# Masks on VectorE, and moved waits (gate tile, boundary, banded buffers, stick scores), in a two-layer hybrid decoder kernel

## The chip, the cores and the metric

The kernel runs on one core of a Trainium2 chip as one launch. The metric is the time of that launch on the device in microseconds (us). The core has TensorE (PE in the profile, its weight loads PEld), VectorE (DVE), ScalarE (ACT), GpSimd (POOL), and SyncE (SP), which here issues the loads of the weights. Each engine works through its own queue in order and waits at semaphores for the others.

## The reference

Two layers over 512 tokens of width 1024, float32. Each layer mixes tokens in three branches and then has an MLP:

```python
h = rms_norm(x, g_mix_pre);  proj = h @ w_in
o_a = mla_branch(...) @ w_o_mla            # 8 heads, causal: key <= query
o_b = swa_branch(...) @ w_o_swa            # 8 heads, window of 128 keys, one sink per head
o_c = stick_breaking_branch(...) @ w_o_sb  # 8 heads, key < query
mixed = gates[0] * o_a + gates[1] * o_b + gates[2] * o_c
x = x + rms_norm(mixed @ w_out, g_mix_post)
x = x + rms_norm(square(relu(rms_norm(x, g_mlp_pre) @ w_up)) @ w_down, g_mlp_post)
```

In the causal branch `s = where(key <= query, s, -inf)` and a softmax over the keys. In the banded branch a query sees the keys of its own block of 128 up to itself, and of the block before it those less than 128 away; the softmax has the exponential of the sink in its denominator. The masks of these two branches are what the change moves.

## The kernel before, in words

**Layout and precision.** Activations lie transposed, channels on the 128 partitions and the 512 tokens along the row. Each float32 matrix product is made of three passes over rounded operands (`three`): high with high, low with high, high with low. The high half of an operand is a copy in the rounded type (`..._hi`, ScalarE), the low half is what the copy lost, a subtraction on VectorE (`..._lo`). Weights come in chunks of 128 x 1024: a load, then `split` on ScalarE (L1053) and on VectorE (L1600). One output tile of 128 x 512 is 24 matmuls of 512 columns (`tile`, 8 steps over k of three passes each).

**What sets the order.** Nothing is planned at run time: the function `order()` at the head of the file lists the tiles in TensorE's order, which gives each tile its PSUM bank by turns (a few banks rotate) and each weight chunk its place in the ring. A tile waits for the release of the bank by the tile that had it before (`take_bank`, `free_of`). Apart from that list each engine's program is written out by hand; the change edits these by hand too.

**Causal heads.** For each head h: TensorE makes the scores, keys on the partitions and queries along the row, in the causal shape only (1280 columns in three banks: 512, 512 and 256), and adds the mask at the end of each bank by a matmul of the identity with a constant (`causal_mask`, L604; the mask is -BIG above the diagonal). VectorE takes the maximum over the key blocks (`biggest`, L1711 and L1713), GpSimd reduces it over the partitions, TensorE subtracts it from the scores (`mla_shift`), ScalarE takes the exponentials (`soft_exp`, L1137) and copies the high half (`soft_hi`, L1144), VectorE makes the low half (`probs_lo`, L1690), and TensorE multiplies with the values (`values`, which wait for the low half). The denominator comes out of the same matmul as further rows of the bank `pv_bank`; ScalarE takes ln and exp of it (L1108, L1110), VectorE multiplies (`soft_out`, L1722, writes `of` and gives the bank free). TensorE's order in round h is: scores of h+1, query projection of h+2, values of h, then a tile of 24 matmuls (a gate tile in most rounds) in whose middle the maximum of h+1 is subtracted. VectorE's order in round h is: maximum h+1, query of h+2, `soft_out` h, a weight split, in layer 0 a part of the angles of the rotary table (`angle_turns`, `angle_less`, `angle`, `angle_ahead`, after heads 0 to 3), low half h+1, scaling of a gate tile. After head 4, in layer 0, ScalarE makes the sines of that table (`table_sin`, with two table loads).

**Banded heads.** The eight heads run in four pairs (t = 0 to 3), with TensorE's scores of a whole pair made together (`band_scores`): two banks a head, 512 and 384 columns, masks of 512 columns for the first and of 256 and 128 for the second, for each head of the pair. Two buffers hold the exponentials (`bs_f`), one each the high and the low half (`bp_hi`, `bp_lo`). The denominator is the sum with the sink on VectorE (`band_den`, L1803), then as above. Beside it run output tiles (`o`), the rotation of the next queries (`rope_in`, `rope_turn`: L1776, L1781, L1788, L1791, L1793) and the scaling of the stick-breaking inputs (`stick_scaled`). The values of a head wait for the bank `pv_bank`, which the head before gives free with its `of`.

**Stick-breaking heads** follow. Their first step is `stick_scores(0)` on TensorE, then the clamp on VectorE (`stick_min`, L1840), and exponentials, logarithms and sums on the way to `stick_tail`.

**Boundary.** At the end of layer 0 the last down tiles are made in halves of 256 tokens. `down_part` adds a tile to `y` (L1964) and squares it for the norm (`gather`, L1616, with a square of ScalarE, L1070), while the first tiles of layer 1 start as soon as banks and inputs are free.

## Time and profile before

| | |
|---|---|
| three runs | 1720.91 us median, 1720.56 to 1721.05 |
| profiled execution, its own time | 1720.57 us |
| its span | 1718.8 us |
| TensorE busy | 1693.2 us, 99% |
| VectorE busy | 1117.5 us, 65% |
| ScalarE busy | 852.8 us, 50% |
| GpSimd busy | 150.8 us, 9% |
| granted TensorE clock, mean | 0.998 |

The span is the profiled execution from its first to its last instruction; its own time is a little more. Busy times count the instructions that do work; matmuls are pipelined, so that two starts of 512 columns lie 0.23 us apart although one takes 0.39 from start to end. L12 is line 12 of the kernel. In a timeline a row may stand for several instructions of a line (x2), and the bracket tells how long the engine was idle before it and what ended that.

### The profile page before, as it was taken

To read this page: it belongs to the slowest core of one execution; us is meant where nothing else is said; L and a number is where in the kernel's file an instruction comes from. 1 tells how busy PE (TensorE), PEld (TensorE's weight loads), DVE (VectorE), ACT (ScalarE), POOL (GpSimd) and SP (SyncE) were. 2 spreads that over 40 slices of the span, in tenths; PEclk is the share of its full clock that TensorE was granted. 3 is DMA by queue.
4 is the path that set the end of the run, shared out by engine and by line. 5 is a ranking of instruction groups with operands and counts; after the bars stand their busy time and mean duration, and the time that the engine had idled before them with its cause. 6 is when DMAs were issued, how large, how long until landed. Compare 5 with 4: busy or idle time off the path is not lost.

```text
span 1718.8 us, 21730 instructions
## 1 busy us (share of the span) xinstructions
PE 1693.2 (99%) x8533; PEld 1429.0 (83%) x8533; DVE 1117.5 (65%) x1530; ACT 852.8 (50%) x1204; POOL 150.8 (9%) x142
## 2 busy tenths in 40 slices
PE   8999999999999999999999999999999999999997
PEld 6888888888898888888888888888888988888886
DVE  8887888886566534364597777888754765344545
ACT  7576566665455424131466755666644553231223
POOL 0111211111100000000001111111111000000000
PEclk9999999999999999999999999999999999999999
DMA  4121122222332222222321211122224222222222
GB/s 151 66 71 60 62 69 75 78 74 86 135 111 85 93 94 97 99 98 98 120 83 65 77 62 62 62 74 74 74 92 161 78 90 96 98 98 98 98 98 74
DMA packets 47495, 152.02 MB, mean 88 GB/s; under 512 B 5153, under 2 KB 9633, under 8 KB 47394
## 3 DMA queue, kind: packets, MB, share of 16 engines
q1 hardware_dynamic: 45664, 147.36, 24.7%
q10 hardware_dynamic: 1730, 3.28, 0.5%
q8 instruction: 68, 1.11, 0.3%
q14 instruction: 33, 0.27, 0.0%
HBM read 146.42 MB, written 4.19 MB: 88 GB/s over the span
## 4 chain that ended last, share of the span: by engine, by line
PE 83%; issue 6%; DVE 5%; ACT 3%; POOL 1%; DMA 1%; SPq 0%; DVEq 0%; POOLq 0%; ACTq 0%
PE bank L599 78%; PE bank L604 2%; PE bank L856 1%; PE bank L901 1%; POOL mix L2342 1%; ACT w_hi L1053 1%; DVE w_lo L1600 1%; POOL fb L2372 1%; PE bank L703 0%; DMA x<-in_x 0%; DVE hf L1647 0%; ACT dn L1110 0%; ACT dn L1108 0%; DVE h_lo L1635 0%; DVE of L1722 0%
## 5 line engine op out<-in xcount | busy, mean ns | idle before, releaser
L599 PE MATMUL bank<-h_hi,w_hi 128*128 128x512 f32 (+1 forms) x1224 | 477.3, 390 | 6.4 <-DVEq L1739 2.8
L599 PE MATMUL bank<-h_hi,w_lo 128*128 128x512 f32 (+1 forms) x1224 | 471.9, 386 | 0.0
L599 PE MATMUL bank<-h_lo,w_hi 128*128 128x512 f32 (+1 forms) x1224 | 471.6, 385 | 0.0
L1053 ACT ACTIVATE w_hi<-raw 128x1024 fp32r<-128x1024 f32 (+2 forms) x269 | 270.5, 1013 | 206.4 <-DMA raw<-in_w 205.9
L1600 DVE TENSOR_TENSOR w_lo<-raw,w_hi 128x1024 fp32r<-128x1024 f32 (+2 forms) x269 | 316.3, 1179 | 59.5 <-ACT w_hi L1053 52.7
L599 PEld LDWEIGHTS bank<-h_hi,w_hi 128*128 128x128 f32 x1224 | 230.1, 188 | 55.5 <-issue 6.2
L599 PEld LDWEIGHTS bank<-h_hi,w_lo 128*128 128x128 f32 x1224 | 229.9, 188 | 47.1
L599 PEld LDWEIGHTS bank<-h_lo,w_hi 128*128 128x128 f32 x1224 | 230.2, 188 | 44.8 <-issue 1.2
L599 PE MATMUL bank<-u_hi,w_hi 128*128 128x512 f32 (+1 forms) x560 | 208.0, 371 | 0.0
L599 PE MATMUL bank<-u_hi,w_lo 128*128 128x512 f32 (+1 forms) x560 | 207.7, 371 | 0.0
L599 PE MATMUL bank<-u_lo,w_hi 128*128 128x512 f32 (+1 forms) x560 | 207.7, 371 | 0.0
L599 PEld LDWEIGHTS bank<-u_hi,w_hi 128*128 128x128 f32 x560 | 105.5, 188 | 18.3
L599 PEld LDWEIGHTS bank<-u_lo,w_hi 128*128 128x128 f32 x560 | 105.5, 188 | 18.2
L599 PEld LDWEIGHTS bank<-u_hi,w_lo 128*128 128x128 f32 x560 | 105.5, 188 | 18.0
L1934 DVE TENSOR_TENSOR usq<-relu 128x512 f32<-128x512 f32 x64 | 44.2, 691 | 101.7 <-ACT relu L1258 101.2
L1258 ACT ACTIVATE relu<-bank 128x512 f32<-128x512 f32 x48 | 28.6, 595 | 136.5 <-PE bank L599 136.5
L1952 DVE TENSOR_TENSOR y<-bank,y 128x512 f32<-128x512 f32 x32 | 22.1, 691 | 98.7 <-PE bank L599 98.7
L599 PE MATMUL bank<-o_hi,w_hi 128*128 128x512 f32 x192 | 76.6, 399 | 0.0
L1260 ACT ACTIVATE u_hi<-relu 128x512 fp32r<-128x512 f32 x64 | 40.5, 633 | 70.1 <-DVE relu L1929 68.6
L599 PE MATMUL bank<-o_hi,w_lo 128*128 128x512 f32 x192 | 75.0, 390 | 0.0
L2342 POOL TENSOR_TENSOR mix<-mix,gate 128x512 f32<-128x512 f32 x32 | 44.4, 1390 | 346.5 <-DVE gate L1909 346.5
L599 PE MATMUL bank<-o_lo,w_hi 128*128 128x512 f32 x192 | 74.8, 390 | 0.0
(267 smaller groups left out, 2738.7 us busy)
## 6 DMA issues: line engine op xcount, KB each, us to landing
raw<-in_w SPq DMA_DIRECT2D x251, 512.0 KB, 3.2
x<-in_x SPq DMA_DIRECT2D x16, 256.0 KB, 3.5
side_raw<-in_w SPq DMA_DIRECT2D x6, 512.0 KB, 4.9
x_spill<-x ACTq DMA_DIRECT2D x8, 256.0 KB, 2.2
x<-x_spill SPq DMA_DIRECT2D x8, 256.0 KB, 3.0
out_y<-x SPq DMA_DIRECT2D x8, 256.0 KB, 2.1
raw<-in_w SPq DMA_DIRECT2D x8, 192.0 KB, 2.4
raw<-in_w SPq DMA_DIRECT2D x8, 128.0 KB, 2.3
```

Source lines behind the costliest of these rows:

```text
L599: mm = pe.matmul(o, s, m, start=start and i == 0 and j == 0, stop=last and i == n - 1 and j == 2, skip_group_check=True)
L604: return pe.matmul(o, stationary, moving, start=False, stop=True, skip_group_check=True)
L856: return pe.matmul(to[:, off + col:off + col + w], a, m, start=(r, n, i) in STICK_STARTS, stop=i == 2, skip_group_check=True)
L901: mm = pe.matmul(pv_bank[:, q0:q0 + w], v[:, j, h % 2, :], part[:, s], start=i == 0 and part is p_hi, stop=part is p_lo, skip_group_check= ...
L1053: act.activation(chunk_in(gc, w_hi, side_hi)[:, 0:w], chunk_in(gc, raw, side_raw)[:, 0:w], ACT.Copy)\
L1258: act.activation(relu[:, n % 2, :], tile_bank(name)[:, :], ACT.Relu).then_inc(free_of(name), 1)
L1260: act.activation(u_hi[g % 2][:, t, :], relu[:, n % 2, :], ACT.Square).then_inc(u_h.sem, 1)
L1600: dve.tensor_tensor(chunk_in(gc, w_lo, side_lo)[:, 0:w], chunk_in(gc, raw, side_raw)[:, 0:w], chunk_in(gc, w_hi, side_hi)[:, 0:w].bitcast( ...
L1934: dve.tensor_tensor(usq[:, n % 2, :], relu[:, n % 2, :], relu[:, n % 2, :], ALU.mult)\
L1952: ins = dve.tensor_tensor(y[:, t, :], tile_bank(name)[:, :], y[:, t, :], ALU.add)
L2342: pool.tensor_tensor(mix[:, t, :], mix[:, t, :], gated_at(b, t), ALU.add).then_inc(mix_add.sem, 1)
L2372: pool.tensor_tensor(to, to, tri01[:, :], ALU.mult).then_inc(z_mask.sem, 1)
```

## The change

- **Masks.** In causal heads the mask matmul of the first bank goes. The first maximum is taken in two steps, 128 columns with the mask added and a copy of 384. After the exponentials VectorE takes the minimum of the first 128 columns with a constant `bound`, which is 0 where a key is later than the query and large elsewhere (`causal_masked`), and ScalarE's high half waits for it (`p_mask`). In banded heads half of the mask columns go (512 to 256 in the first bank; the 256-column masks in the second), the first two maxima add the mask, and `band_masked` takes the minimum over two stretches of 256 columns.
- **Gate tile.** The tile ("gate", 0, 2) is taken before the last of four value tiles; `mla_shift(0)` stands before its k-tile 6 in place of 4. The queues of ScalarE and VectorE follow: `split` of the next gate chunk after head 0's halves, scaling of the gate tile before them.
- **Banded buffers.** `bp_hi` and `bp_lo` become two each, the low half written over the exponentials. ScalarE's high half of the odd head moves ahead of the rotation and the stick inputs. VectorE's minimum and low half of the odd head move into `rope_turn`, ahead of its last subtraction, and with that ahead of the stick scaling and of the denominator of the even head.
- **Stick scores.** `stick_scores(0)` is issued inside the tile ("stick_vt", 0), after its first k-tile, and no longer before it.
- **Boundary.** At the end of layer 0 the sum of tile (5, half 1) stays in its place on VectorE, its `gather` moves behind `layer_lo(0, 0)`, and ScalarE's part of it behind the second `next_in`.

```diff
 order():                                       # TensorE's tiles
-        elif h == 1:
-            seq += values[-1:]
         if 0 < h < HEADS - 1:
             seq += own("gate", 0, h + 1)
+        if h == 1:
+            seq += values[-1:]
...
+        bound = place("bound", [P, 2 * P], F32)
-        bp_hi = place("bp_hi", [P, BANDED_COLS], F32R, r3 + 5632)
-        bp_lo = place("bp_lo", [P, BANDED_COLS], F32R, r3 + 9216)
+        bp_hi = [place(f"bp_hi{s}", [P, BANDED_COLS], F32R, r3 + 5632 + 3584 * s) for s in range(2)]
+        bp_lo = [place(f"bp_lo{s}", [P, BANDED_COLS], F32R, r3 + 16896 * s) for s in range(2)]
+        bp_lo_last = place("bp_lo_last", [P, BANDED_COLS], F32R, r1 + 16384 + 10240)
...
 PE, scores():
-                            causal_mask(to, off, b, MASK_CAUSAL).then_inc(score_full.sem, 1)
+                            if b:
+                                mm = causal_mask(to, off, b, MASK_CAUSAL)
+                            mm.then_inc(score_full.sem, 1)
 PE, band_scores():
-                                    mm = add(band[r][0][:, :].rearrange("p (a c) -> p a c", a=2), cst[:, IDENT, :],
-                                             both.unsqueeze(1).broadcast_to([P, 2, 2 * P]))
+                                    mm = add(band[r][0][:, 2 * P:4 * P], cst[:, IDENT, :], both)
                                 else:
-                                    add(band[r][1][:, 0:2 * P], cst[:, IDENT, :], both)
                                     mm = add(band[r][1][:, 2 * P:3 * P], cst[:, IDENT, :], cst[:, MASK_CAUSAL, :])
 PE, order of the work:
+                    tile(("gate", 0, 2), h_hi, h_lo, None, lambda: mla_shift(0), half=KT - 2)
                     mla_v(NB - 1)
-                    tile(("gate", 0, 2), h_hi, h_lo, None, lambda: mla_shift(0))
...
-                    stick_scores(0)
-                    tile(("stick_vt", 0), h_hi, h_lo)
+                    tile(("stick_vt", 0), h_hi, h_lo, None, lambda: stick_scores(0), half=1)
 ACT, soft_exp() and soft_hi():
-                        act.wait_ge(*p_l(n if n <= HEADS else n - 1))
+                        act.wait_ge(*(pv_full(n - 1) if n > HEADS + 1 else p_l(min(n, HEADS))))
...
+                    act.wait_ge(*p_mask(n + 1))
+                    read = n - 1 if n > HEADS else n
+                    if read > 0:
+                        act.wait_ge(*pv_full(read))
 ACT, start of the heads:
-                    mla_q(1)
-                    mla_v(NB - 1)
                     for j in range(NB - 1):
                         mla_v(j)
+                    mla_q(1)
                     soft_exp(0)
+                    mla_v(NB - 1)
+                    soft_hi(0, s_f[:, :], p_hi[:, :])
                     split(C["gate", 0, 2] + 2)
-                    soft_hi(0, s_f[:, :], p_hi[:, :])
 ACT, banded pairs:
                         sink_exp(n)
+                        band_hi(n + 1)
                         if t < 2:
                             rope_out(t + 3, wq_hi[:, t + 2, :])
...
-                        band_hi(n + 1)
 DVE, biggest():
-                            ins = dve.tensor_scalar(to[:, q0:q0 + w], src, floor, None, ALU.max)
+                            ins = dve.scalar_tensor_tensor(out=to[:, q0:q0 + w], in0=src, scalar=floor, in1=both,
+                                                           op0=ALU.max, op1=ALU.add)
                         elif i == 0:
-                            ins = dve.tensor_copy(to[:, q0:q0 + w], src)
+                            dve.tensor_tensor(to[:, 0:P], src[:, 0:P], cst[:, MASK_CAUSAL, :].bitcast(F32), ALU.add)
+                            ins = dve.tensor_copy(to[:, P:SEQ], src[:, P:SEQ])
+                def causal_masked(h):
+                    dve.wait_ge(*p_exp(banks_of(h) + 1))
+                    dve.tensor_tensor(s_f[:, 0:P], s_f[:, 0:P], bound[:, 0:P], ALU.min).then_inc(p_mask.sem, 1)
+                def band_masked(n):
+                    dve.wait_ge(*p_exp(banks_of(HEADS + n + 1)))
+                    halves = bs_f[n % 2][:, 0:6 * P].rearrange("p (a c) -> p a c", a=3)[:, 0:3:2, :]
+                    dve.tensor_tensor(halves, halves, bound[:, :].unsqueeze(1).broadcast_to([P, 2, 2 * P]), ALU.min)
+                       .then_inc(p_mask.sem, 1)
 DVE, start of the heads:
                     mla_q(1)
+                    mla_v(0)
+                    mla_qk(1)
+                    for j in range(1, NB - 1):
+                        mla_v(j)
+                    causal_masked(0)
+                    scaled(("gate", 0, 2), mix[:, 2, :])
                     mla_v(NB - 1)
-                    mla_qk(1)
-                    for j in range(NB - 1):
-                        mla_v(j)
+                    probs_lo(0, s_f[:, :], p_hi[:, :], p_lo[:, :])
                     split(C["gate", 0, 2] + 2)
-                    probs_lo(0, s_f[:, :], p_hi[:, :], p_lo[:, :])
-                    scaled(("gate", 0, 2), mix[:, 2, :])
 DVE, round h, after the angle operations:
                         if h + 1 < HEADS:
+                            causal_masked(h + 1)
                             probs_lo(h + 1, s_f[:, :], p_hi[:, :], p_lo[:, :])
 DVE, banded pairs:
+                        band_masked(n)
                         band_lo(n)
...
-                            rope_turn(t + 3, ("swa_q", t + 2), wq_lo[:, t + 2, :], wq_hi[:, t + 2, :])
+                            rope_turn(t + 3, ("swa_q", t + 2), wq_lo[:, t + 2, :], wq_hi[:, t + 2, :],
+                                      lambda: second_low(n + 1))      # band_masked, band_lo
+                        else:
+                            second_low(n + 1)
                         if t == 0:
-                            rope_in(4, ("swa_q", 3), 0.125)
-                        elif t < 3:
-                            stick_scaled(0, t - 1)
-                        band_den(n)
-                        band_lo(n + 1)
+                            rope_in(4, ("swa_q", 3), 0.125, lambda: band_den(n))
+                        else:
+                            if t < 3:
+                                stick_scaled(0, t - 1)
+                            band_den(n)
 DVE, end of layer 0:
-                            down_part(HALF, 1)
+                            down_sum(HALF, 1)                          # its gather after layer_lo(0, 0)
```

## Rows read from the trace of the kernel before

**Rows 1.** The page's busy times: us, share of the span, instructions.
```profile
PE 1693.2 (99%) x8533; PEld 1429.0 (83%) x8533; DVE 1117.5 (65%) x1530; ACT 852.8 (50%) x1204; POOL 150.8 (9%) x142
```

**Rows 2.** TensorE's waits: us in total, times, longest us.
```profile
PE bank L599 <- DVE h_lo L1635: 4.0, 4, 1.4
PE bank L599 <- DVEq L1739: 2.8, 2, 1.4
PE bank L599 <- DVE of L1722: 1.9, 6, 0.5
```

**Rows 3.** Timeline of TensorE, gate tile: start us, us, [idle before <-releaser].
```profile
55.19 0.39 PE L599 MATMUL bank<-w_lo,ckn_hi 128*128 128x512 f32 x1
55.42 0.40 PE L599 MATMUL bank<-w_hi,ckn_lo 128*128 128x512 f32 x1
57.22 0.47 PE L599 MATMUL bank<-h_hi,w_hi 128*128 128x512 f32 x1 [1.40 <-DVEq L1739]
```

**Rows 4.** The same timeline, scores of head 2 with the mask.
```profile
88.06 0.22 PE L604 MATMUL bank<-cst 128*128 128x128 f32 x1
88.12 0.39 PE L599 MATMUL bank<-mq_hi,mk_hi 128*128 128x384 f32 x1
88.35 0.34 PE L599 MATMUL bank<-mq_lo,mk_hi 128*128 128x384 f32 x1
```

**Rows 5.** The same, masks of a band pair and the values behind.
```profile
185.74 0.73 PE L604 MATMUL bank<-cst 128*128 128x512 f32 x2
...
187.24 0.68 PE L604 MATMUL bank<-cst 128*128 128x256 f32 x4
188.43 0.36 PE L599 MATMUL bank<-bp_hi,wv_hi 128*128 128x256 f32 x1 [0.51 <-DVE of L1722]
```

**Rows 6.** VectorE's groups by form: busy us, mean ns, idle before us.
```profile
L1934 DVE TENSOR_TENSOR usq<-relu 128x512 f32<-128x512 f32 x64 | 44.2, 691 | 101.7 <-ACT relu L1258 101.2
...
L1690 DVE TENSOR_TENSOR p_lo<-s_f,p_hi 128x1280 fp32r<-128x1280 f32 x16 | 23.9, 1492 | 17.1 <-ACT p_hi L1144 16.8
...
L1690 DVE TENSOR_TENSOR bp_lo<-bs_f,bp_hi 128x896 fp32r<-128x896 f32 x16 | 17.5, 1092 | 6.2 <-ACT bp_hi L1144 6.1
...
L1861 DVE TENSOR_TENSOR later_f<-later_f 64x128 f32<-64x128 f32 x16 | 4.5, 284 | 0.6
```

**Rows 7.** Timeline of VectorE, low halves of heads 1 and 2.
```profile
75.85 1.49 DVE L1690 TENSOR_TENSOR p_lo<-s_f,p_hi 128x1280 fp32r<-128x1280 f32 x1 [0.21 <-ACT p_hi L1144]
...
87.29 1.49 DVE L1690 TENSOR_TENSOR p_lo<-s_f,p_hi 128x1280 fp32r<-128x1280 f32 x1 [0.54 <-ACT p_hi L1144]
```

**Rows 8.** Timeline of ScalarE, high half of head 1.
```profile
74.47 1.27 ACT L1144 ACTIVATE p_hi<-s_f 128x1280 fp32r<-128x1280 f32 x1
```

**Rows 9.** Timeline of TensorE, values of head 1.
```profile
79.36 0.40 PE L599 MATMUL bank<-p_hi,mv_hi 128*128 128x512 f32 x1
```

**Rows 10.** Timeline of ScalarE, behind the gate of head 4.
```profile
125.51 1.28 ACT L1058 ACT_TABLE_LOAD   x1
```

**Rows 11.** Timeline of VectorE, banded stage and the first stick clamp.
```profile
176.14 1.09 DVE L1690 TENSOR_TENSOR bp_lo<-bs_f,bp_hi 128x896 fp32r<-128x896 f32 x1 [0.57 <-ACT bp_hi L1144]
...
182.12 0.69 DVE L1793 TENSOR_TENSOR wq_lo<-ra,wq_hi 128x512 fp32r<-128x512 f32 x1 [0.70 <-ACT wq_hi L1170]
184.22 0.69 DVE L1776 SCALAR_TENSOR_TENSOR rp_lo<-bank,rp_hi 128x512 fp32r<-128x512 f32 x1 [1.41 <-ACT rp_hi L1166]
...
203.89 0.69 DVE L1803 TENSOR_TENSOR dn<-bank,dn 64x512 f32<-64x512 f32 x1 [0.67 <-PE bank L599]
...
220.97 0.69 DVE L1682 TENSOR_TENSOR tmp<-bank,rstd_x 128x512 f32<-128x512 f32 x1 [2.43 <-PE bank L599]
...
239.60 0.67 DVE L1840 TENSOR_SCALAR fb<-bank 128x512 f32<-128x512 f32 x1
```

**Rows 12.** Timelines of VectorE and GpSimd, an add beside a reduction.
```profile
167.94 1.05 DVE L1791 TENSOR_TENSOR ra<-ra,rb 128x512 f32<-128x512 f32 x1
...
167.40 1.78 POOL L2331 PARTITION_ALL_REDUCE bmxr<-bmx  x1 [22.53 <-DVE bmx L1713]
```

More of the change, by code:

```diff
@@ L124 @@
 VECS = V_SINK + HEADS
-IDENT, SWAP, NEG_TRI, NEG_ONE, ONE, MASK_CAUSAL, MASK_PREV, NEG_PART, TRI_MOST = range(9)
-N_CONST = 9 * P
+IDENT, SWAP, NEG_TRI, NEG_ONE, ONE, MASK_CAUSAL, MASK_PREV, NEG_PART, TRI_MOST, BOUND = range(10)
+N_CONST = 11 * P
 TRIG = 4 * 4
@@ L453, in banks_of, with band_low @@
             return 3 * n if n < HEADS else 2 * n + HEADS
+        def band_low(n):
+            return bp_lo_last if n == HEADS - 1 else bp_lo[n % 2]
         def chunk_of(name):
@@ L638, in weight, with tile @@
                     return (chunk_in(gc, w_hi, side_hi)[:, rows], chunk_in(gc, w_lo, side_lo)[:, rows])
-                def tile(name, hi, lo, ready=None, halfway=None, cols=ALL):
+                def tile(name, hi, lo, ready=None, halfway=None, cols=ALL, half=KT // 2):
                     c = chunk_of(name)
@@ L647, in tile @@
                             pe.wait_ge(*ready[0](ready[1] + t + 1))
-                        if halfway and t == KT // 2:
+                        if halfway and t == half:
                             halfway()
@@ L727, in scores @@
                         to, off = banks[b]
-                        three(to[:, off + col:off + col + w], [(keys(j), queries(q0, w))], start=off + col == 0)
+                        mm = three(to[:, off + col:off + col + w], [(keys(j), queries(q0, w))], start=off + col == 0)
                         if n + 1 == len(pieces) or pieces[n + 1][3] != b:
-                            causal_mask(to, off, b, MASK_CAUSAL).then_inc(score_full.sem, 1)
+                            if b:
+                                mm = causal_mask(to, off, b, MASK_CAUSAL)
+                            mm.then_inc(score_full.sem, 1)
                 def less_biggest(n, pieces, banks, biggest_):
@@ L1315, in _ @@
                     .then_inc(const_set, 1)
+                act.activation(bound[:, :], cst_f[:, BOUND * P:(BOUND + 2) * P], ACT.Copy).then_inc(const_set, 1)
                 table_sin(2, QPE, 2, slice(HEAD, P))
@@ L1714, in biggest @@
                         ins.then_inc(mx_step.sem, 1)
+                def causal_masked(h):
+                    dve.wait_ge(const_set, 4)
+                    dve.wait_ge(*p_exp(banks_of(h) + 1))
[3 more added lines that the diff above has]
+                    halves = bs_f[n % 2][:, 0:6 * P].rearrange("p (a c) -> p a c", a=3)[:, 0:3:2, :]
+                    dve.tensor_tensor(halves, halves, bound[:, :].unsqueeze(1).broadcast_to([P, 2, 2 * P]), ALU.min)\
+                       .then_inc(p_mask.sem, 1)
                 def soft_out(n):
@@ L1766, in mla_biggest, with rope_in @@
                     biggest(h, CAUSAL, score, mx)
-                def rope_in(n, name, scale):
+                def rope_in(n, name, scale, between=None):
                     dve.wait_ge(*rp_h(n + 1))
@@ L1778, in rope_in @@
                            .then_inc(rp_l.sem, 1)
+                    if between:
+                        between()
                     if n:
@@ L1782, in rope_in, with rope_turn @@
                                              op0=ALU.mult, op1=ALU.mult).then_inc(free_of(name), 1)
-                def rope_turn(n, name, dst, hi):
+                def rope_turn(n, name, dst, hi, between=None):
                     dve.wait_ge(*rot(n + 1))
@@ L1791, in rope_turn @@
                     dve.tensor_tensor(ra[:, :], ra[:, :], rb[:, :], ALU.add).then_inc(rp_sum.sem, 1)
+                    if between:
+                        between()
                     dve.wait_ge(*rpo_h(n + 1))
@@ L1836, in stick_min @@
                             dve.wait_ge(*p_l(2 * HEADS + max(h - 1, 0)))
+                            if h == 0:
+                                dve.wait_ge(*pv_full(2 * HEADS - 1))
                             if h < 2:
@@ L1965, in down_part @@
                        .then_inc(free_of(name), 1)
+                def down_part(t, h):
+                    down_sum(t, h)
                     gather(MPOST, t, h)
@@ L2306, in layer_lo, with first_lo_gather @@
                         next_lo(t, (4 + h) * KT + t + 1, vec(V_PRE + t, layer=now[0] + 1), HALVES[h])
+                    def first_lo_gather(t, h):
+                        layer_lo(t, h)
+                        if t == 0:
+                            gather(MPOST, HALF, 1)
                     for p in range(KT // 2 + 1):
-                        residual(p, 0, KT, layer_lo if more else None)
+                        residual(p, 0, KT, (first_lo_gather if p == 1 else layer_lo) if more else None)
                         if p == 0:
-                            down_part(HALF, 1)
+                            down_sum(HALF, 1)
+                            if not more:
+                                gather(MPOST, HALF, 1)
                         elif p == 1:
```

27 lines of the change are left out of this document (18 added, 9 removed).

## The prediction, made before the changed kernel was seen

> **What bounds the kernel now.** I read four views in this order. First the busy times of the page: TensorE is at work for 1693.2 of 1718.8 us [rows 1], so it is the bound almost everywhere, and an edit gains only by taking columns off TensorE or by ending one of its waits. Then the waits of TensorE by releaser [rows 2]: the reader is to see that they are few and short: 2.8 us in two waits behind VectorE's L1739 (the gate tile, one a layer), 1.9 us in six behind the head output of L1722 (banded stage), 4.0 us in four behind L1635, the longest of 1.4 us at the boundary between layers. All that this change aims at is in those rows and in the mask matmuls. Third the timeline of TensorE at these places [rows 3 to 5]. Last, VectorE's and ScalarE's queues around a head [rows 6 to 11], because the change moves work onto VectorE and makes ScalarE wait for it; there it must be seen how much idle time VectorE has before the operation that TensorE waits for.
>
> The sum is made against the profiled execution: 1720.57 us, span 1718.8 and 1.8 around it. The median of the runs shown is 1720.91, 0.3 more, which I leave out.
>
> **The gate tile.** In both layers TensorE starts the last value matmul at 55.42 and the gate tile at 57.22: 1.80 where 0.23 is the pace (55.19 to 55.42) [rows 3], so 1.57 lost, and some 0.07 of restart. With the order swapped the tile takes the bank that is free and the value matmul the one freed late, by then long free. Gain 1.64 a layer at that point. What hides the moved work: `shift(0)` moves from before k-tile 4 to before k-tile 6, where its maximum is ready. The price is in VectorE's queue: the scaling of the gate now stands before the low half of the probabilities of head 0, and a weight split of 1.2 us behind it, so head 1's work on VectorE starts some 0.3 to 0.6 later than before, while TensorE comes 1.64 earlier.
>
> **Causal masks, TensorE's side.** The mask of bank 0 starts at 88.06 and the next matmul at 88.12, 0.06; the 384-column matmul behind it takes 0.23 to the next [rows 4], where three quarters of the 0.23 of 512 columns are 0.17: some 0.05 for the switch. 0.11 a head, 0.88 a layer, 1.76 for 16.
>
> **Causal masks, the other side.** The first maximum becomes a masked add of 128 columns and a copy of 384, about 0.2 more on VectorE. The new minimum on 128 columns costs 0.29 (L1861) [rows 6]. What counts is its place: ScalarE's high half now waits for it, and it stands in VectorE's queue behind the weight split and, in layer 0, behind the angle operations of heads 1 to 4. In the trace of before those ran beside ScalarE's high half: for head 1 it ran from 74.47 to 75.74 [rows 8], VectorE's last angle operation ended at 75.64, and the low half started at 75.85 after 0.21 idle [rows 7]. After: angle operation to 75.64, minimum to 75.93, high half 1.27, low half at about 77.3, so 1.45 later, and 0.3 more from the queue of the gate tile: 1.75. Low half to 79.1; TensorE wants it at 79.36 less 1.97 of lead (1.64, and three masks) = 77.4 [rows 9]. The lead is gone at head 1, stall 1.7.
>
> Heads 2, 3 and 4 repeat it, since VectorE goes from head to head almost without idle time: each adds the high half and the minimum less the idle time VectorE had before the low half (0.54 at head 2 [rows 7]; heads 3 and 4 repeat the pattern of head 1 with as little), so 1.1, 1.5 and 1.5. VectorE is 1.75 + 4.1 = 5.9 late at head 4. TensorE had 2.0 of slack there (low half of head 1 ended at 77.34, wanted at 79.36 [rows 7, 9]), but in the next round ScalarE stands with two table loads and the sines from 125.51 on [rows 10] behind the gate, right before the exponentials of head 6, and that stretch had no slack: the lateness passes whole. Term for layer 0's causal stage, gate gain and mask cuts in it: bounds +3.8 (the slack holds) and +6.3, and below nothing if the lead survives (−2.5, a rival below). I take +6.0.
>
> In layer 1 there are no angle operations. The minimum costs 0.3 beside the exponentials, the gate queue's 0.4 stays. TensorE stalls some 0.4 once and then keeps the rest: −1.64 − 0.88 + 0.4 = −2.15; bounds −2.5 and 0.
>
> **Banded stage.** TensorE loses masks: of two 512-column and four 256/128-column ones (0.73 and 0.68 [rows 5]) some 0.5 a pair, 4 us in all by name. But each pair's next matmul waits for `of` anyway (0.51 at 188.43 [rows 5]), a chain over the denominator on VectorE, so I credit none of it by itself. On that chain stand, new: the minimum of 512 elements, 0.61 from start to start (0.69 alone, L1934 [rows 6]), twice a pair, ScalarE's high half of 0.95 behind each, and the low half of 1.09 [rows 6], which now stands *before* the denominator and not after it. The idle time in VectorE's queue pays a part.
> - Pair 0: the low half of band head 0 started at 176.14 [rows 11]; now the minimum ends at 176.1, high half to 177.1, low half 1.05 later. Then, before the low half of the rotated query, 0.70 of idle time at 182.12 goes and 0.61 + 1.0 + 1.02 come: 3.0 later in all. The idle 1.41 before 184.22 [rows 11] pays half, and one operation of 0.6 to 0.7 moves behind the denominator. Denominator at 186.3 for 185.54: +0.76 at the head's `of`, on which TensorE stands.
> - Pair 1: +1.5 at the even low half and the same 1.9 behind it, paid by the idle 0.67 before 203.89 [rows 11], and by the odd high half that no longer delays the denominator's exponential on ScalarE: +1.4.
> - Pair 2: the same, but VectorE had 2.43 idle at 220.97 [rows 11]: +0.36.
> - Pair 3: both low halves stand before the denominator and `of`, behind which stick-breaking's first clamp starts: 239.60 [rows 11] becomes 243.3. The stick chain behind it has waits of its own, and I let it pay a little over half, as in pair 0: +1.70, bounds 0 and +3.7.
>
> The moved stick scores (inside the tile, after its first k-tile) take a 0.6 wait of TensorE away before that last step, so it only changes where the same lateness is felt: zero; bounds −0.6 and 0. Double buffers let the exponentials and the high half start earlier, but the low half still waits for the minimum, which waits its turn: zero by itself. Sum of the stage: +4.2 a layer, 8.5 for both. Bounds: −1.5 a layer (VectorE hides all, the 1.9 of `of` waits [rows 2] go) and +5.5.
>
> **Boundary.** The wait at L1635 of 1.4 us [rows 2] ends when a down tile's sum is done; the change moves one gather, whose square comes from ScalarE, out from ahead of it. Bounds 0 and −1.4; I take −0.6, once.
>
> **Start-up.** One more copy of 256 columns on ScalarE and 128 KB more of constants, before the first matmul needs either: 0, bounds 0 and +0.3.
>
> **Sum.** 6.0 − 2.15 + 8.5 − 0.6 = +11.8: 1720.57 + 11.8 = 1732.4 us.
>
> **One rule against it.** The row: an add of two SBUF inputs (L1791) that started at 167.94, 0.54 after GpSimd's reduction of 167.40, took 1.05 where its kind takes 0.69 [rows 12, 6]; so it was slowed by 0.36, yet ended inside the reduction's 1.78. Both inputs of the banded minimum are in SBUF, and for even heads it would start 0.4 to 1.2 us into such a reduction. As a mechanism of this kernel: 4 such minima a layer, each 0.36 to 1.2 later, on the denominator's chain, 8 × 0.36 = 2.9 to 8 × 1.2 = 9.6, of which part stays in slack: 1735 to 1741 us.
> The Trainium skill, page "SBUF — State Buffer", section "SBUF: two separate sides", says that VectorE and GpSimd share a pair of ports under an exclusive lock, and that a VectorE operation with two SBUF inputs is fully blocked while a GpSimd operation that reads SBUF holds it. By that rule the add of 167.94 would have ended no earlier than 169.2 + 0.7; the trace has 168.99, so it agrees in direction and not in size.
>
> **Rivals.**
> - *VectorE hides the masks* (faster). If the low halves stay inside the 2.0 us of slack at head 1 and in the banded stage's idle times, TensorE keeps everything: −3.3 gate, −1.8 causal masks, −4 band masks and `of` waits at most, −0.6: 1711 to 1713 us. For it: VectorE is busy 65% on average. Against it: at heads 1 and 2 of layer 0 it was idle for 0.21 and 0.54 before the low half [rows 7], less than one high half. It decides at the low half of head 1: if that starts before 76 us, this one holds.
> - *The band stage is neutral* (slower, less). The low half before the denominator costs nothing because double buffers pull the exponentials ahead; then 6.0 − 2.15 − 0.6 = +3.3, 1723.8. For it: pair 2's idle of 2.43. Against: the minimum waits for its turn in VectorE's queue.
> - *Layer 0 keeps the slack*: 3.8 for 6.0, 1730: inside the forecast's own range.
> - *The ports*, above: 1735 to 1741.
> - *The change doesn't do what it says*: the waits move and the masks' cost equals their gain, 1720 to 1721.5.
>
> **Chances.** Forecast with its own range of 1726 to 1737: 0.62. Neutral band stage 0.14. Ports 0.11. VectorE hides it 0.09. No change 0.04. The range takes in the forecast, most of the neutral band stage and the lower part of the ports: 1723 to 1738. Faster by over 0.2% (3.4 us, about what can be told from no change): 0.09; within it: 0.07 (0.04, and 0.03 from the low end of the neutral band stage); slower: 0.84.
>
> **What would show it.** Right: the low half of head 1 starts at 77 or later, and TensorE's waits have new rows behind `p_lo` L1690 in layer 0 alone, some 8 us in all; no wait behind L1739; waits behind `of` grow from 0.5 to over 1 us; the first clamp is 3 to 4 us late against the values of band head 6. Wrong: `p_lo` waits absent or the denominators at their old distance from the band scores. If the causal stage of layer 0 is no longer than before, the queue of angle operations was misjudged; if the clamp is not late, the banded chain was.

## The result and the profile after

The changed kernel takes 1749.47 us (median of 4 runs, 1748.81 to 1750.73) against 1720.98 for the kernel before on the same chip (4 runs, 1720.56 to 1721.65): ratio 1.0167, 95% interval 1.0155 to 1.0179, or 28.5 us slower. Forecast were 11.8 us. The profiled execution is the one of 1750.73 us, span 1748.9; the one of before had 1718.8. So the two traces lie 30.1 us apart, and the sums below are made between them.

The page's busy times and TensorE's waits after (us in total, times, longest), which answer to [rows 1] and [rows 2]:

```profile
PE 1701.2 (97%) x8501; PEld 1434.5 (82%) x8501; DVE 1133.1 (65%) x1578; ACT 853.9 (49%) x1205; POOL 151.0 (9%) x142
...
PE bank L605 <- DVE of L1746: 12.1, 6, 2.8
PE bank L605 <- DVEq L1763: 5.6, 2, 3.0
PE bank L605 <- DVE h_lo L1644: 2.8, 3, 1.8
PE bank L605 <- DVE bp_lo L1699: 2.6, 2, 1.4
PE bank L610 <- DVE sp_lo L1903: 2.5, 2, 1.2
PE bank L605 <- DVE mix L1691: 2.4, 1, 2.4
```

The waits for the head output went from 1.9 to 12.1 us, those behind the query's release from 2.8 to 5.6, and three groups are new. TensorE's busy time has also grown, by 8.0 us, with 32 matmuls less. The granted clock tells why. The next fence is TensorE's timeline at the tile gate(0, 3) of layer 0, and then a table by stretches (us; busy time and count of PE, PEld, DVE, ACT, POOL; granted clock; DMA share; GB/s):

```profile
70.51 0.77 PE L605 MATMUL bank<-h_hi,w_hi 128*128 128x512 f32 x1 [2.59 <-DVEq L1763]
...
71.00:76.00 5.00, 5.00 (x13) 3.87 (x12) 4.42 (x7) 3.48 (x7) 0.59 (x1) 0.50 0.00 0
78.00:80.00 2.00, 2.00 (x11) 1.65 (x10) 0.80 (x1) 1.97 (x3) 0.00 (x0) 1.00 0.00 0
200.00:202.00 2.00, 2.00 (x9) 1.81 (x8) 1.33 (x4) 0.19 (x1) 1.36 (x1) 0.50 0.00 0
```

After a wait of 2.59 us the granted clock is 0.50 for 5 us, that is 1.2 GHz and not 2.4, and then 1.00 again. That is so too behind the wait of 2.43 us for the head output at 198.77.

**Where the 30.1 us went.** I matched the same matmuls in both traces and took how much later each starts. The column on half clock is what the lateness grew by from the first to the last matmul of each stretch at half pace (0.43 us from start to start for 512 columns and 0.21 for 256, where 0.23 and 0.12 are the pace). The first matmul behind a wait is in it, so some tenths of it are restart and not clock.

| stage | later at its end | gained in it | of that half clock | the rest | forecast |
|---|---|---|---|---|---|
| layer 0, causal heads (to 164.9 of before) | 8.9 | 8.9 | 2.9 | 6.0 | 6.0 |
| layer 0, banded and stick (to 258.3) | 19.8 | 10.9 | 4.3 | 6.6 | 4.2 |
| to the heads of layer 1 (902.3) | 19.2 | -0.6 | 0 | -0.6 | -0.6 |
| layer 1, causal heads (1014.1) | 21.9 | 2.8 | 1.6 | 1.2 | -2.15 |
| layer 1, banded and stick (1107.5) | 30.2 | 8.3 | 1.6 | 6.7 | 4.2 |

Of the 16.7 us between the forecast and the measured loss the two banded stages are the greater part: 19.2 us were lost there where 8.5 were forecast.

### The profile page after: what moved, and what is told of

Same layout as the page of the kernel before. It is cut to its first block, busy times and chain, and to the rows that moved or that the text cites. A ratio compares the mean times of both kernels' runs of the same rounds, so it can differ in the third digit from the quotient of the medians.

```text
span 1748.9 us, 21737 instructions
## 1 busy us (share of the span) xinstructions
PE 1701.2 (97%) x8501; PEld 1434.5 (82%) x8501; DVE 1133.1 (65%) x1578; ACT 853.9 (49%) x1205; POOL 151.0 (9%) x142
## 3 DMA queue, kind: packets, MB, share of 16 engines
q8 instruction: 68, 1.11, 0.3%
## 4 chain that ended last, share of the span: by engine, by line
PE 66%; issue 9%; DVE 9%; ACT 6%; POOL 1%; DMA 0%; DVEq 0%; POOLq 0%; ACTq 0%
PE bank L605 63%; ACT w_hi L1058 1%; PE bank L610 1%; ACT bp_hi L1151 1%; DVE w_lo L1609 1%; PE bank L862 1%; PE bank L907 1%; POOL mix L2395 1%; DVE bp_lo L1699 1%; DVE bmx L1719 1%; DVE dn L1831 1%; ACT p_hi L1151 1%; POOL fb L2425 0%; ACT dn L1115 0%; DVE mx L1726 0%
```

## The experiments

Each run has its own runs of the kernel before on the same chip (medians 1720.4 to 1720.9). The ratio is given with its 95% interval.

| run | what it is | median us | ratio |
|---|---|---|---|
| e1 | changed, gate tile part undone | 1747.67 | 1.0153 [1.0138, 1.0168] |
| e2 | changed, masks on TensorE | 1722.30 | 1.0010 [1.0000, 1.0019] |
| e3 | changed, old banded order | 1757.12 | 1.0209 [1.0193, 1.0224] |
| e4 | changed, TensorE kept busy in the banded waits | 1745.46 | 1.0143 [1.0128, 1.0158] |
| e5 | changed, masks on TensorE and gate part undone | 1718.47 | 0.9987 [0.9978, 0.9996] |
| e6 | before with the gate part alone | 1725.92 | 1.0031 [1.0019, 1.0042] |
| e7 | before with one load later | 1724.64 | 1.0023 [1.0014, 1.0032] |
| e8 | e5 with causal masks on VectorE | 1726.22 | 1.0034 [1.0022, 1.0046] |
| e9 | e5 with banded masks on VectorE | 1739.71 | 1.0108 [1.0095, 1.0122] |
| e10 | e8, minimum ahead of the angles | 1720.22 | 0.9997 [0.9988, 1.0006] |
| e11 | e9, odd minimum earlier | 1729.94 | 1.0051 [1.0038, 1.0065] |
| e12 | e5, query of head 1 between the maxima | 1717.03 | 0.9977 [0.9968, 0.9986] |
| e13 | e9, TensorE kept busy | 1734.28 | 1.0079 [1.0064, 1.0094] |
| e14 | e11, denominator before the odd low half | 1722.98 | 1.0018 [1.0008, 1.0027] |

The parts put together: e5 is -2.3 us against its runs of before, causal masks (e8 less e5) +7.75, banded masks (e9 less e5) +21.2, gate tile in their company (changed less e1) +1.8. The sum is 28.5, the measured loss 28.5. That they agree to the tenth is chance: e1's four runs lie between 1743.95 and 1749.44, and the intervals of e1 and of the changed kernel overlap. What is tested by it is that causal and banded masks add up: e5 and both costs give 1747.5, and e1, which has both, took 1747.67. The gate part does not add up. It costs 1.8 us beside both masks (e1), 3.8 without them (e2 less e5) and 5.2 alone in the kernel before (e6).

### The gate tile: e1, e6, e7

e1 takes the part out of the changed kernel, e6 puts it alone into the kernel before; the diff is that of the part shown above, undone or done.

> The changed kernel with its gate tile part undone (order of the tiles, place of the maximum, queues of ScalarE and VectorE at the start of the heads); all other parts stay. Theory: the swap keeps the value chunk of the weights in use until after the gate tile, the next chunk's load starts 6 us later, and through VectorE's queue the tile gate(0,3) of each layer waits 2.6 to 3.0 us for its bank, after which TensorE ran at half clock for 5 to 6 us. Undoing it takes away about +3.2 of lag at that place in layer 0 and +2.9 in layer 1: 1743 to 1744 us. Rival: the gate swap gains its 1.6 a layer as I forecast and the lateness comes from the masks in VectorE's queue: then undoing it costs, 1751 to 1753 us.

> The kernel before with the gate tile part alone (tile order, place of the maximum, the queues at the start of the heads). Theory: the 1.57 us wait goes and a longer one comes at gate(0,3), with half clock behind it in some executions: +2.5 and +1.3 us, 1723.5 to 1726 us. Rival (my forecast): -1.6 a layer, 1717.7 us.

e7 is the kernel before with one wait on SyncE:

```diff
                         sp.wait_ge(*full(LAST[gone % CHUNKS] + 1))
+                        if gone % CHUNKS == C["mla_v",]:
+                            sp.wait_ge(*shift(1))
```

> The kernel before with one wait more on SyncE: the load that takes the place of the value chunk of the weights waits until head 0's maximum is subtracted (about 5 us later than before, where the changed kernel starts it). Nothing else is moved. Theory: the late load alone makes VectorE's split late, with it the maxima of head 1 and the query of head 2, whose bank gate(0,3) waits for: a wait of 1.5 to 3 us appears behind the query's release (L1739) at 69.6 and at its place in layer 1: 1724 to 1729 us. Rival: it is the changed order of VectorE's queue and not the load: 1720.5 to 1722 us.

Alone the part costs 5.2 us (e6), where the forecast had a gain of 3.3. Why stands in the trace of the changed kernel; first the loads of weights with their first and last start between 50 and 70 us, before and after, then ScalarE's and VectorE's timelines after:

```profile
L582 SPq DMA_DIRECT2D raw<-in_w x4: 327/328/432, 55.8 to 67.9; - x4
```

```profile
L588 SPq DMA_DIRECT2D raw<-in_w x4: 328/379/431, 61.8 to 66.1; - x4
...
65.14 1.06 ACT L1058 ACTIVATE w_hi<-raw 128x1024 fp32r<-128x1024 f32 x1 [1.54 <-DMA raw<-in_w]
...
66.23 1.23 DVE L1609 TENSOR_TENSOR w_lo<-raw,w_hi 128x1024 fp32r<-128x1024 f32 x1 [1.11 <-ACT w_hi L1058]
...
69.63 0.68 DVE L1761 TENSOR_TENSOR mqf<-bank,tab 128x512 f32<-128x512 f32 x1
```

The load of the next weight chunk started at 55.8 and now at 61.8. It goes into the place in the ring that the value chunk leaves, and SyncE waits for the last tile that reads it. That is the last value tile, which the swap puts behind the gate tile's 24 matmuls. ScalarE then stands 1.54 us for the load and VectorE 1.11 for ScalarE, the maxima of head 1 and the query of head 2 come 1.4 us later, and gate(0, 3) uses the bank of that query (two banks rotate): TensorE, 1.6 ahead, waits 2.59 where it waited for nothing. e7, which only starts that load later, costs 3.9 us without any other edit, as the theory had it in size. It missed the place: the wait of 1.53 us stands at the key matmul of head 2, behind the gate tile's scaling (`mix`), which in e7 still stands at its old place in VectorE's queue. So the late load by itself is shown to cost most of what e6 costs. That in the changed kernel it works through the bank of head 2's query is read from the trace above; no run has the new queue without the late load. The half clock is on top: e6's trace has it behind both of its long waits, e7's behind none.

In the changed kernel the part costs only 1.8 (e1), less than the expected 5.5 to 6.5, and its rival, that undoing the part costs, fell too. In layer 0 the later waits of the masks, which are for the same engine, take the lateness in: the changed kernel's trace is 3.3 us behind e1's at 80 us and 1.0 behind at 105. In layer 1 it is 4.1 behind at the end of the causal heads and 1.3 at the end of the banded stage, where e1 had two stretches of half clock (1.6 and 2.9 us) and the changed kernel one (1.6). So a part of the small 1.8 is chance of the clock.

### The masks: e2, e5, e8, e9

e2 puts all masks back on TensorE in the changed kernel; e5 undoes the gate part too; e8 and e9 are e5 with one kind of mask on VectorE.

> The changed kernel with all masks on TensorE again (causal and banded), no minimum on VectorE and no wait of ScalarE for it; gate swap, banded buffers and order, stick scores and boundary stay. Theory: masks on VectorE cost about 8 us in layer 0's causal heads and some 4 us in the banded stages; the rest is the gate tile and the banded order: 1735 to 1739 us. Rival: the masks are the whole loss: 1718 to 1722 us. Second rival: they cost nothing, 1748 to 1754 us.

> The changed kernel with the masks back on TensorE and the gate tile part undone; what is left of the change is banded buffers and order, stick scores and boundary. Theory: masks on TensorE brought 1722.3, and the gate tile there still cost 2.5 us in layer 0 and 1.3 in layer 1 at the first head after it, so without it 1718 to 1719 us: a version under the kernel before. Rival: the gate tile's lateness is made up later in any case: 1720.5 to 1722.5 us.

> As the one with neither masks on VectorE nor gate tile part, but with the causal masks of bank 0 on VectorE. Theory: layer 0's angle operations with the minimum behind them cost 6 to 8 us there, layer 1 costs 0 to -1: 1724 to 1727 us. Rival: the lateness is the maxima's (two steps for one) and comes in both layers alike: 1720 to 1722 us in all, or the same in both layers.

> As the version with neither masks on VectorE nor gate tile part (1718.5), but with the banded masks on VectorE. Both masks together on it gave 1747.7 and the causal ones 1726.2. Theory: the parts add up, so the banded masks alone cost some 21 us, about 10.7 a layer, of which 3 to 4 a layer are half clock behind the long waits for the head output: 1738 to 1741 us. Rival: the two only cost that much together, because the causal masks make the banded stage start late: under 1733 us.

My expectation for e2 fell and its rival stood: the masks are the whole loss. What is left of the change without them and without the gate part is a gain of 2.3 us (e5). The causal masks cost 7.75 us (e8), all in layer 0. At the end of its causal heads e8's trace is 7.9 us behind that of the kernel before, 1.6 of them a stretch of half clock at 121.7, and over the causal heads of layer 1 the lag is 6.7 at the start and at the end. The low halves tell why. In layer 1 of the kernel before VectorE was idle for 1.5 to 2.1 us ahead of those of heads 1 to 7, more than the 1.39 it is idle in e8, so the round trip to ScalarE fits in. At heads 1 to 4 of layer 0 it had 0.15 to 0.54. The banded masks cost 21.2 (e9), and by themselves: beside the causal ones they cost the same (e1 less e8, 21.45).

### Where the causal minimum stands: e10

```diff
                             split(C["swa_q", 0] + 2)
+                        if h + 1 < HEADS:
+                            causal_masked(h + 1)
                         if now[0] == 0:
                             if h == 0:
                                 angle_turns(1)
...
                         if h + 1 < HEADS:
-                            causal_masked(h + 1)
                             probs_lo(h + 1, s_f[:, :], p_hi[:, :], p_lo[:, :])
```

> The version with the causal masks alone on VectorE (1726.2), with the minimum moved ahead of the angle operations of layer 0 in VectorE's queue, behind the weight split. Theory: the 7.9 us of layer 0 come from the high half that waits behind the angles; with the minimum ahead it starts 0.3 after the exponentials and runs beside the angles again: 1717.5 to 1719 us. Rival: the minimum and the longer maxima are what VectorE's queue can't hold in layer 0, wherever they stand: 1722 us or more.

6.0 of the 7.75 us go with the place of one operation of 0.29 us, the half clock behind the wait of 2.37 us among them. VectorE's timeline at head 1, e8 and then e10, which answers to [rows 7]:

```profile
75.98 0.43 DVE L1586 TENSOR_SCALAR tt<-tt 128x512 f32<-128x512 f32 x1
76.44 0.29 DVE L1733 TENSOR_TENSOR s_f<-s_f,bound 128x128 f32<-128x128 f32 x1
78.12 1.49 DVE L1702 TENSOR_TENSOR p_lo<-s_f,p_hi 128x1280 fp32r<-128x1280 f32 x1 [1.39 <-ACT p_hi L1154]
```

```profile
75.07 0.28 DVE L1733 TENSOR_TENSOR s_f<-s_f,bound 128x128 f32<-128x128 f32 x1
...
76.82 1.49 DVE L1702 TENSOR_TENSOR p_lo<-s_f,p_hi 128x1280 fp32r<-128x1280 f32 x1
```

In e8 the low half starts 1.39 us after VectorE is free, behind ScalarE's high half; in e10 the high half ran beside the angles and the low half waits for nothing. 1.75 us stay, and the expected 0 did not come: half a microsecond in head 4's round and 1.2 at the values of head 6 of layer 0. What makes these is open; the longer maxima (0.28 + 0.55 for 0.68) are my guess.

### Where the banded minimum and low half stand: e3, e11, e14

e3 is the changed kernel with the old order on VectorE and ScalarE (the odd head's minimum and low half after `band_den`, its high half after the rotation); e11 is e9 with the odd minimum ahead of `mixed`; e14 is e11 with the denominator first:

```diff
 e11
+                        band_masked(n + 1)
                         mixed(n + 1)
...
                 def second_low(n):
-                    band_masked(n)
                     band_lo(n)
 e14, besides
-                            rope_turn(t + 3, ("swa_q", t + 2), wq_lo[:, t + 2, :], wq_hi[:, t + 2, :],
-                                      lambda: second_low(n + 1))
-                        else:
-                            second_low(n + 1)
+                            rope_turn(t + 3, ("swa_q", t + 2), wq_lo[:, t + 2, :], wq_hi[:, t + 2, :])
...
                             band_den(n)
+                        band_lo(n + 1)
```

> The changed kernel with the old order of the banded pairs: VectorE takes the odd head's minimum and low half after the rotation, the stick scaling and the even head's denominator, ScalarE the odd high half after rotation and stick inputs; masks stay on VectorE, buffers stay double. Theory: the waits of TensorE behind the head output (2.4 to 2.8 us, two a layer) come from the denominator standing behind the odd low half; undone, they fall under 1 us and the half clock behind them goes: 10 to 14 us less, 1736 to 1740 us. Rival: the minimum itself makes the lateness, wherever it stands: 1746 us or more.

> The version with the banded masks alone on VectorE, with the odd head's minimum moved ahead of the mixing of the output tile, so that ScalarE's high half is done when VectorE comes to the low half. Theory: the round trip (1.07 us idle before each low half) at the odd heads goes, four a layer, and the waits for the head output become shorter by 1 us each: 5 to 9 us under the banded masks alone, clock included. Rival: the even heads' round trip and the work itself make the lateness: 0 to 3 us less.

> The version with the banded masks on VectorE and the odd head's minimum early (1729.9), with the even head's denominator taken before the odd head's low half. Theory: since the high half is ready early, the low half no longer idles VectorE, and the 1.0 us of it ahead of the denominator is what is left of the waits for the head output: 3 to 6 us less, 1724 to 1727 us. Rival: as with the late minimum (where the old order cost 7.6 more), the low half after the denominator makes the next head late: 1730 to 1735 us.

VectorE's timeline in the first pair of the changed kernel, to be held against [rows 11]:

```profile
184.37 1.16 DVE L1737 TENSOR_TENSOR bs_f<-bs_f,bound 128x512 f32<-128x512 f32 x1
186.61 1.09 DVE L1699 TENSOR_TENSOR bp_lo<-bs_f,bp_hi 128x896 fp32r<-128x896 f32 x1 [1.07 <-ACT bp_hi L1151]
...
191.81 0.68 DVE L1737 TENSOR_TENSOR bs_f<-bs_f,bound 128x512 f32<-128x512 f32 x1
193.57 1.09 DVE L1699 TENSOR_TENSOR bp_lo<-bs_f,bp_hi 128x896 fp32r<-128x896 f32 x1 [1.07 <-ACT bp_hi L1151]
194.58 0.68 DVE L1821 TENSOR_TENSOR wq_lo<-ra,wq_hi 128x512 fp32r<-128x512 f32 x1
195.18 0.68 DVE L1800 SCALAR_TENSOR_TENSOR rp_lo<-bank,rp_hi 128x512 fp32r<-128x512 f32 x1
195.90 0.69 DVE L1831 TENSOR_TENSOR dn<-bank,dn 64x512 f32<-64x512 f32 x1
...
197.95 0.68 DVE L1746 TENSOR_TENSOR of<-bank,dn 64x512 f32<-64x512 f32 x1 [0.64 <-ACT dn L1115]
```

Each low half stands 1.07 us after VectorE is free, and this is so at all of them: the minimum, then ScalarE's 0.95, then the low half, nothing between. The odd head's three steps (191.81 to 194.58) stand ahead of the denominator at 195.90, for which TensorE waits. With the odd minimum early (e11) the round trip runs beside other work and 9.8 us go, a little over what was expected; the waits for the head output fall from 12.2 us in e9 to 5.9. With the denominator ahead of the low half too (e14) another 7.0 go, more than expected, and the banded masks cost 4.5 us more than e5. But these 7.0 are not where I looked for them. TensorE's waits in e11 and then in e14:

```profile
PE bank L605 <- DVE of L1744: 5.9, 6, 1.3
PE bank L610 <- DVE sp_lo L1900: 1.2, 2, 0.6
```

```profile
PE bank L605 <- DVE of L1744: 5.6, 6, 1.3
```

The waits for the head output are hardly shorter. Of the 5.6 us between the two traces 3.1 are at the start of the stick-breaking heads, where two waits of 0.6 a layer (behind `sp_lo` and `tmp`) are gone, and 1.6 are a stretch of half clock in layer 1 that e11 had behind a wait of 1.28 us. So what the old order is worth here is the last pair, whose denominator the stick chain stands behind.

e3 fell and its rival stood: with the late minimum the old order is worse by 7.6 us. As I read it, the round trip then stands after the denominator and ahead of the head output, and the next pair's maxima are behind it; the waits for the head output grow from 12.1 to 14.3 us, and e3's trace has eight stretches of half clock among the heads where the changed kernel's has five. The order was right for the late minimum and wrong for the early one.

### The clock: e4, e13

e4 is the changed kernel and e13 is e9, both with this ahead of three values of each layer; what it computes is overwritten:

```diff
+                    if n in (HEADS + 1, HEADS + 3, HEADS + 5):
+                        take_bank(("o", 0, n + 1 - HEADS))
+                        for _ in range(8):
+                            pe.matmul(tile_bank(("o", 0, n + 1 - HEADS))[:, :], cst[:, ONE, :], cst[:, 0:4, :],
+                                      start=True, stop=True, skip_group_check=True)
                     pe.wait_ge(*p_l(n + 1))
```

> The changed kernel with eight more matmuls of 512 columns (1.8 us) ahead of the values of band heads 1, 3 and 5, into the bank that the next output tile overwrites; they compute nothing that is used. Theory: the long waits there lower TensorE's clock to half for 3 to 6 us afterwards, and a TensorE that works through most of the wait keeps its clock: the half-speed stretches behind the band heads go, 5 to 8 us less: 1742 to 1745 us. Rival: only the waits cost and the clock's fall has another cause: no gain, 1749 to 1752 us.

> The version with the banded masks alone on VectorE (1739.7), with eight more matmuls of 512 columns (1.8 us) ahead of the values of band heads 1, 3 and 5, into the bank that the next output tile overwrites; they compute nothing that is used. Theory: of the 21 us, 5 to 7 are half clock behind the long waits for the head output, and TensorE at work through the wait keeps its clock: 1733 to 1735 us. Rival: the clock's share is small and the added matmuls cost as much as they save: 1738 to 1741 us.

More work made both faster, e4 by 4.0 us (1745.46, just over the expected 1742 to 1745) and e13 by 5.4. The span and mean granted clock of e9 and of e13, each with TensorE's wait for the head output in e13:

```profile
core 0: 1736.7 us, clock 0.994
```

```profile
core 0: 1732.2 us, clock 0.997
...
PE bank L605 <- DVE of L1749: 2.1, 4, 0.5
```

The waits are only filled, not shorter in sum (12.2 us of waits for the head output in e9; 2.1 and 48 matmuls of 0.23 in e13), and the time still falls: what went is the half clock behind them. e9's trace has three stretches of it in the banded stages, 1.6, 2.9 and 1.5 us by the lag, and e13's none among the heads. So of the 21.2 us of the banded masks 5 to 6 are clock (5.4 between the medians, 4.9 when each is taken against its own runs of before, 6.0 by the lag). It can't be added to the 9.8 and 7.0 above, which shorten the same waits.

### A version under both kernels: e12

```diff
-                    mla_biggest(0)
-                    mla_q(1)
+                    mla_biggest(0, lambda: mla_q(1))     # between steps 2 and 3 of the maximum
```

> The version with neither masks on VectorE nor gate tile part (1718.5), with one operation moved: VectorE takes the query of head 1 between the second and third step of the maxima of head 0, which frees the bank of the gate tile. Theory: the wait of 1.4 us behind L1739 comes down to some 0.5 a layer, nothing else is late by it since the reduction of head 0 has 0.5 us of slack: 1716.5 to 1717.5 us. Rival: the later reduction stops TensorE at the subtraction and gives the gain back: 1718 to 1719 us.

It takes 1717.03 us, as expected: with e5's parts and this move 0.23% under the kernel before, and under the changed one by 32 us. The wait behind the query's release is 0.9 us in two, where [rows 2] have 2.8.

## Why the prediction was wrong, step by step

The direction was right, the size was not: 11.8 us for 28.5, outside the range. Three steps of the sum failed: the gate tile, the slack of the banded stage, and the clock, which had no term.

1. **Gate tile.** Failed. "The tile takes the bank that is free": it did, the wait at [rows 3] is gone. The step that failed is that I looked at banks and at queues of VectorE, and not at what the swap does to SyncE: a weight chunk is in use until its last tile, so moving the last value tile moved a load by 6 us. The sign that I gave, no wait behind L1739, failed too: behind the same line, now L1763, there are 5.6 us. I had -1.64 a layer, alone it is +2.6 a layer (e6).
2. **Causal masks, layer 0.** The mechanism was right: e10 shows that it is the place behind the angles, and the low half of head 1 starts at 79.20 where the forecast had 77 or later. That the sum came out (+6.0 forecast, 6.0 without the clock) is in part luck. It held a gain of 1.64 from the gate that did not come, and the masks' own cost without clock was about 6.2 (7.75 in e8, 1.6 of it half clock) and not the 7.6 that this leaves. The sign for it failed too: 8 us of waits behind the causal low half were forecast, and there were 1.4 in two. I took the low half as the first thing that TensorE waits for; it waited longer (2.36 us at 122.14) for the gate tile's scaling behind the low half, which frees a bank for the keys of head 6. The slack of 2.0 us [rows 7, 9] was read at the wrong consumer.
3. **Causal masks, layer 1.** Forecast was -2.15, of which -1.64 were the gate's; it was +2.8. The masks by themselves give about nothing (e8), and the rest is the gate's wait of 3.03 us with its half clock (1.6).
4. **Banded stage.** The mechanism was right, the low halves stand ahead of the denominator and each waits for a round trip, the term was mis-sized: 4.2 a layer, measured 6.6 and 6.7 without clock. The step that failed is the slack. Pair 0's own terms, 3.0 late less half of 1.41 less the 0.65 of the operation that moves, leave 1.6, and 0.76 was entered; pair 3's 3.7 was entered as 1.7 because "the stick chain behind it has waits of its own". No row stood behind either cut. Without the clock, and less the masks that TensorE saved, pair 0 cost 1.5, pair 1 1.8 in layer 0 and 2.1 in layer 1 (for 1.4), pair 2 0.1 to 0.2 (for 0.36), and pair 3 with the stick chain 3.1 to 3.3. The sign for it held nearly: the first clamp is 20.9 us later than before (260.47) and the values of band head 6 18.1 (251.59), 2.8 between them where 3 to 4 were forecast. Why the idle time paid so little is not shown.
5. **The clock.** Missing. No wait of TensorE in the trace of before was over 1.6 us and, from 5.7 us to the last few, its granted clock was 1.00; the changed kernel's waits were up to 3.0. About 10 of the 30 us are half clock (the table's column adds up to 10.4), and e4 and e13 show by 4.0 and 5.4 us that it can be had back. The forecast priced a wait by its length alone.
6. **Boundary.** Right: -0.6, at the wait that was at 858.64 before.
7. **Stick scores, buffers.** Priced at zero together with the lateness; e5 shows them and the boundary as -2.3 in all.

Of the rivals the ports played a small part. Of the sixteen minima two took 1.16 us, those that started 0.42 into GpSimd's reduction (184.37, and its like in layer 1); three that started 1.25 to 1.51 us into one took 0.69, as did all others. That is 0.9 us in all. The Trainium skill, page "SBUF — State Buffer", section "SBUF: two separate sides", would have blocked the first until the reduction's end at 185.73; it ended at 185.53, so as with [rows 12] only the direction agrees.

## What to carry to other kernels

An operation of 0.3 us moved to another engine costs by the place it takes in that engine's queue: put it where its operands become ready, ahead of work that can run beside what waits for it, and it cost 1.75 us and not 7.75. When tiles are reordered, list for each resource of the moved tile (bank, weight place in the ring, the load behind it) who gives it free and who waits for that. And price a long wait of TensorE at more than its length: behind 26 of 33 waits of 2.1 to 3.0 us half clock took another 1.5 to 3.0 us here.

## What the runs showed of the hardware

In the changed kernel's trace TensorE had seven waits of over 2.3 us among the heads. After five of them (2.59, 2.43, 2.44, 3.03 and 2.80 us) its granted clock was 0.50, that is 1.2 GHz, for a while; after two (2.36 at 122.14 and 2.38 at 1061.11) it stayed at 1.00. In the traces of the changed kernel and of all the experiments, from 20 to 1700 us, there are 33 waits of 2.1 to 3.0 us, and half clock stands behind 26 of them. Each such stretch cost 1.5 to 3.0 us of lag.

Shorter waits are not free of it. Of 60 waits of 1.0 to 1.6 us in these traces and that of the kernel before, six were followed by half clock: one of 1.42 us in e9, three of 1.28 to 1.33 in e11, and two of 1.34 and 1.07 in e14. The same waits of 1.34 and 1.07 us were not followed by it in layer 1 of e14, and the wait of 2.36 us in round 4 of the causal heads was not in the changed kernel and was in e4. So the length of one wait does not settle it, and these runs do not show what does. e14 at 189 to 193 us, behind its wait of 1.34 (columns as above):

```profile
189.20:192.40 3.20, 3.20 (x12) 2.81 (x12) 2.38 (x6) 1.03 (x2) 1.78 (x1) 0.50 0.00 0
```

Some of these kernels spread more from run to run: e1's four runs lie between 1743.95 and 1749.44, e14's ten between 1722.20 and 1727.82, while e5's eleven lie within 1.4 us. But the changed kernel's four, with five such stretches in its trace, lie within 2 us. The Trainium skill, page "TensorE: Matmul & The Clock Gate", section "HAM oscillation — how this bites in real kernels", tells of waits for DMAs that throttle TensorE between blocks of matmuls, so that the next block starts slow; the traces here agree in kind, with shorter waits, of 1.07 to 3.03 us and for VectorE.
